# A hybrid decoder step on one core: 320 instead of 344 columns in the RG-LRU, state updates of HGRN2 over 128 stacked rows, and cached keys scored two blocks at a time with a ring of eleven

## The chip, the core and the metric

One core of one Trainium2 chip (trn2) runs the whole program. The metric is the device time of one execution in microseconds.

## What is computed

A four-layer trunk runs over one prompt of 256 tokens and over eight sampled sequences of 8 tokens, 320 columns in all, with the model dimension 1024 and everything in float32. Layers 0 and 3 have an RG-LRU mixer, layer 1 an SSD mixer, layer 2 an HGRN2 mixer; behind each mixer stands a cross attention of 4 heads into 256 memory tokens. For the prompt the memory's keys and values are computed here; for the eight samples they are read from a cache (`cache_mem_k`, `cache_mem_v`). What the change touches, cut from the reference:

```python
# causal_conv: y is the sum of four taps over the columns and the state of 3 columns in front
uu = jnp.concatenate([state, u], axis=1)
y = b + sum(w[k] * uu[:, k:k + L] for k in range(4))
# rglru_mixer, 2048 channels in 8 blocks of 256
r = sigmoid(blocks(u) @ w_a + b_a)
i = sigmoid(blocks(u) @ w_x + b_x)
log_a = -8.0 * r * softplus(-lam)
a = exp(log_a)
b = sqrt(-expm1(2.0 * log_a)) * (i * u)
h = scan(h_t = a_t * h_(t-1) + b_t)         # from h0 for each sequence
y = (h * silu(gate)) @ w_out
# gla_chunked of hgrn2_mixer, 16 heads, key and value dimension 128; for a sample of 8 tokens one chunk
G = cumsum(log_f)
o = causal(q exp(G) (k exp(-G))^T) v + q exp(G) S
S = S * exp(G_last) + (k * exp(G_last - G))^T v
# memory_cross_attn
p = softmax(q mem_k^T / 16)
y = (p mem_v) @ w_o
```

## The kernel before

**Layout.** The columns 0 to 255 (SEQ) are the prompt, 256 to 319 the samples, sequence by sequence; NT is 320. Inside the RG-LRU and the SSD there is a second layout of 347 columns, in which each sample sequence has its 3 columns of convolution state in front of it (SEG = 11 columns a sequence). CV is 344, the width over which the convolution and what follows it run in that layout.

**Weights.** SyncE (SP) brings each weight block (8 x 256 columns for all 128 partitions) into one of 4 slots of `raw`, four DMAs each (`put`), and waits for a slot to come free. ScalarE rounds it to fp32r halves `wh` (line 1613), GpSimd makes the remainder `wl` (line 1593, eight instructions a block). TensorE makes every projection as three fp32r products, high x high (line 751), low x high (line 752) and high x low (line 756), of 320 columns each, 8 chunks deep. Each engine's program is written out by hand, in the order in which the lines stand, and the engines wait for each other by counting semaphores. `did` counts an instruction of VectorE's own, `sync` waits until the counted ones have ended.

**RG-LRU.** A layer has 8 groups of 256 channels. TensorE's loop takes for each group the gate (`take_gate`, which waits for VectorE's line 2300 to have read the gate before), u (`take_u`), and the two fp32 gate products of the convolved u for the group before (`take_ri`, line 842: 8 products of CV columns, 16 records; it waits for the end of the convolution, `rg_conv_done`, and for the packed state output to be read), then `turn_pack`, which transposes the new states. VectorE runs `conv` (line 2284 the first tap, line 2288 the other three, two instructions a tap), `gate` (2300), `update` (2304, 2306), `scan` (2312 to 2320), `product` (2329 for the 256 prompt columns, 2330 for the 64 sample columns, which it gathers from the layout with gaps) and `o_low` (2332 on). ScalarE does the sigmoids (lines 1690 to 1716), Exp, Ln and the rounding of the output. The copy to a transposed output is read at line 2133 (`outs`).

**HGRN2.** A layer has 8 groups, each a pair of heads. TensorE takes g, q, f and v of group i (`take_g`, `take_q`, `take_f`, `take_v`) and between them works on group j = i - 1. `turn_and_score` makes transposes of the keys (bank 5), and the scores (line 1209). `turn_back` (line 1202) transposes on and waits for VectorE's copy of the keys. The state of the eight samples of a head is updated by

```python
def gain(i, h, half):
    if half == 0:
        pe.wait_ge(*past("hg_vm_ready", i * 2 + (h + 1)))
    if i + h + half:
        pe.wait_ge(*past("hg_sn_read", i * 4 + (2 * h + half)))
    v = hg_vm[64:P, 4 * half:4 * half + 4, :]
    pe.matmul(ps[:, 7, :], hg_kt[64:P, 2, :], v, start=True, stop=True).then_inc(S("hg_sn_full"), 1)
```

an fp32 product over the 64 sample rows, of 4 sequences x 128 columns; the trace has two records for one such product. `hg_vm` holds the v of the 64 tokens laid out by sequence with zeros elsewhere (VectorE, lines 2630 to 2635), `hg_kt` the keys turned to rows, copied out of PSUM (line 2604). VectorE adds each gain to the decayed state (`new_state`, 2623 to 2628; `hg_sn_read` counts them). TensorE's order in one iteration is take_g, take_q 0, turn_and_score 0, take_q 1, turn_back 0, gain(j,0,0), take_f 0, outputs and last_state of head 0, take_f 1, turn_and_score 1, gain(j,0,1), take_v 0, turn_back 1, take_v 1, gain(j,1,0), outputs and last_state of head 1, take_v 2, gain(j,1,1), sums. ScalarE (from line 1935) reads the projections: line 1956 for one of q's and k's sources, 1975 and 1976 for v, and the exponentials in between. VectorE then has masks, blocks of v, sums of logs, keys, new states, `finish` (2637) and the gate in that order (loop at 2714 to 2750).

**Attention.** The 16 cached key blocks of a layer (128 tokens x 1024, two for each of 8 samples) and then its 16 value blocks come by one DMA of 512 KB each into a ring of 12 buffers, `at_kb`; load n waits for `at_kb_used` of n - 12. Six of the ring's first seven are loaded early (`EARLY`), the seventh (`kb5`) behind `h_ready`, the other five with the query weights. TensorE turns each key block in 8 transposes (line 1427), ScalarE and VectorE copy four each into one of two buffers `at_kbt`, and the block's 8 score products (32 rows each, 128 columns, line 1437, two records each) stand behind the transposes of the next block:

```python
for n in range(1, 16):
    turn_cache(n)
    cache_scores(n - 1)
    if n in (5, 6, 11, 12):
        prompt_turn(n // 8, (n - 5) % 6)
cache_scores(15)
```

Then the values are multiplied with the probabilities, 4 products a block (line 1505), and SP loads the last four value blocks as the first four are used. SP also stores the prompt's new keys (`store_keys`).

## Time and profile before

| | |
|---|---|
| time, median of 3 runs (range) | 2144.67 us (2142.47 to 2145.44) |
| the profiled execution's own time | 2145.3 us |
| its span in the trace | 2143.4 us |
| mean granted TensorE clock | 0.963 |
| DMA | 324.36 MB, mean 151 GB/s |

The trace shows when each instruction of each engine ran, what it read and wrote by the program's names, and, where its engine stood idle before it, which instruction released it. PE is TensorE, DVE VectorE, ACT ScalarE, POOL GpSimd. A line in the order of time is a run of like instructions: the start of the first, the time from it to the end of the last (instructions of one engine overlap somewhat), the number, and in brackets the idle time before the first and its releaser. PEclk is the granted TensorE clock as a share of the full 2.4 GHz. An fp32 product of TensorE has two records in the trace, an fp32r product one.

### The profile page before, as it was taken

Reading aid. Unit: us, or ns where it says so; the run is one execution under the profiler, and the core shown is the slowest. Engines: PE = TensorE matmul, PEld = TensorE weight load, DVE = VectorE, ACT = ScalarE, POOL = GpSimd, SP = SyncE. Lnnn points to the kernel's source line nnn. Section 1 sums busy time; section 2 is a strip of 40 time slices with the busy share of each in tenths; the row PEclk is TensorE's granted clock in tenths of the full one; section 3 lists DMA queues with packets and bytes.
Section 4 is the critical chain, followed back from the end, with each engine's and each line's share of the span. In section 5 each row is a group of like instructions: output and inputs, shape, how many; then the busy total and the mean of one; then the engine's idle time right before and its main releaser. Section 6 shows DMA issues by size and latency. Waiting matters only on the chain.

```text
span 2143.4 us, 35491 instructions
## 1 busy us (share of the span) xinstructions
PE 2010.6 (94%) x13874; PEld 1788.5 (83%) x13874; DVE 1242.6 (58%) x2220; ACT 905.9 (42%) x1501; POOL 994.8 (46%) x1245
## 2 busy tenths in 40 slices
PE   5898999998999999999999999998999999989987
PEld 4887989698888898897898888887898888879966
DVE  6688442426787777744256566666354147873443
ACT  3476522333544444333353343333242347663332
POOL 4667705036445554150365455555432347665602
PEclk8999999999999999999999999999899999999997
DMA  4443466635434445475452344444386344435850
GB/s 126 132 136 125 133 214 229 213 99 163 117 109 132 134 133 153 161 256 189 131 169 75 112 130 125 135 136 135 103 289 205 135 147 132 142 119 168 280 203 25
DMA packets 331590, 324.36 MB, mean 151 GB/s; under 512 B 21560, under 2 KB 312288, under 8 KB 331424
## 3 DMA queue, kind: packets, MB, share of 16 engines
q1 hardware_dynamic: 330560, 321.75, 47.0%
q8 instruction: 111, 1.82, 0.3%
q10 hardware_dynamic: 864, 0.34, 0.1%
q14 instruction: 55, 0.45, 0.1%
HBM read 292.41 MB, written 29.61 MB: 150 GB/s over the span
## 4 chain that ended last, share of the span: by engine, by line
PE 63%; DVE 25%; ACT 5%; issue 3%; DMA 2%; SPq 1%; POOL 0%; ACTq 0%; DVEq 0%
PE ps L751 9%; PE ps L752 9%; PE ps L756 8%; PE ps L1361 5%; PE ps L1370 4%; DVE work L2288 3%; DVE work L2133 2%; PE ps L741 2%; DVE work L2418 2%; PE ps L1427 2%; PE ps L742 2%; PE ps L743 2%; PE ps L1168 2%; PE ps L1444 1%; PE ps L1474 1%
## 5 line engine op out<-in xcount | busy, mean ns | idle before, releaser
L1593 POOL TENSOR_TENSOR wl<-raw,wh 128x256 fp32r<-128x256 f32 x1216 | 990.3, 848 | 1115.1 <-ACT wh L1613 1114.7
L751 PE MATMUL ps<-Hh,wh 128*128 128x320 f32 x1280 | 400.2, 326 | 25.2 <-DVE Hl L2172 12.2
L1613 ACT ACTIVATE wh<-raw 128x1024 fp32r<-128x1024 f32 x304 | 311.8, 1053 | 193.4 <-PE ps L756 52.9
L752 PE MATMUL ps<-Hl,wh 128*128 128x320 f32 x1280 | 385.2, 314 | 0.0
L751 PEld LDWEIGHTS ps<-Hh,wh 128*128 128x128 f32 x1280 | 246.2, 192 | 48.5 <-issue 24.2
L752 PEld LDWEIGHTS ps<-Hl,wh 128*128 128x128 f32 x1280 | 246.7, 193 | 1.5
L2133 DVE TENSOR_SCALAR work<-ps 128x512 f32<-128x512 f32 (+9 forms) x236 | 108.1, 474 | 208.1 <-DMA out_rgh_s<-work 50.9
L756 PE MATMUL ps<-Hh,wl 128*128 128x320 f32 x1280 | 215.1, 310 | 0.0
L756 PEld LDWEIGHTS ps<-Hh,wl 128*128 128x128 f32 x1280 | 196.1, 189 | 0.0
L751 PE MATMUL ps<-Oh,wh 128*128 128x320 f32 x512 | 156.8, 318 | 3.7 <-DVE Ol L2859 3.7
L752 PE MATMUL ps<-Ol,wh 128*128 128x320 f32 x512 | 155.6, 316 | 0.0
L741 PE MATMUL ps<-Oh,wh 128*128 128x320 f32 x400 | 126.3, 316 | 3.5 <-POOL wl L1593 1.4
L2190 DVE TENSOR_TENSOR work<-work 128x320 f32<-128x320 f32 x80 | 41.1, 514 | 143.4 <-ACT work L2099 112.4
L742 PE MATMUL ps<-Ol,wh 128*128 128x320 f32 x400 | 123.9, 310 | 0.0
L743 PE MATMUL ps<-Oh,wl 128*128 128x320 f32 x400 | 123.8, 309 | 0.0
L1361 PE MATMUL ps<-work,raw 128*128 128x256 f32 x512 | 113.8, 379 | 0.0
L1370 PE MATMUL ps<-raw,work 128*128 128x256 f32 x512 | 113.3, 379 | 0.0
L1370 PEld LDWEIGHTS ps<-raw,work 128*128 128x128 f32 x512 | 96.8, 190 | 13.5
L1361 PEld LDWEIGHTS ps<-work,raw 128*128 128x128 f32 x512 | 96.5, 190 | 13.5
L751 PEld LDWEIGHTS ps<-Oh,wh 128*128 128x128 f32 x512 | 99.7, 195 | 4.9 <-DVE Ol L2859 4.8
L752 PEld LDWEIGHTS ps<-Ol,wh 128*128 128x128 f32 x512 | 99.5, 194 | 0.0
L842 PE MATMUL ps<-work,raw 128*128 128x344 f32 x256 | 81.4, 472 | 15.9 <-DVE work L2133 15.3
(412 smaller groups left out, 3809.4 us busy)
## 6 DMA issues: line engine op xcount, KB each, us to landing
raw<-rg_w_in SPq DMA_DIRECT2D x128, 256.0 KB, 3.6
raw<-hg_w_in SPq DMA_DIRECT2D x128, 256.0 KB, 4.8
raw<-ssd_w_in SPq DMA_DIRECT2D x96, 256.0 KB, 4.0
work<-cache_mem_k SPq DMA_DIRECT2D x40, 512.0 KB, 6.0
raw<-rg_w_out SPq DMA_DIRECT2D x64, 256.0 KB, 3.5
raw<-x_w_k SPq DMA_DIRECT2D x64, 256.0 KB, 3.6
raw<-x_w_v SPq DMA_DIRECT2D x64, 256.0 KB, 3.5
raw<-x_w_q SPq DMA_DIRECT2D x64, 256.0 KB, 5.4
```

The source lines that it names most:

```text
L741: pe.matmul(out, high(*wi), mh, start=start, stop=False)
L742: pe.matmul(out, high(*wi), ml, start=False, stop=False)
L743: return pe.matmul(out, low(*wi), mh, start=False, stop=stop)
L751: pe.matmul(ps[:, bank, 0:n], high(half, k), mh[:, k, 0:n], start=(k == 0), stop=False)
L752: pe.matmul(ps[:, bank, 0:n], high(half, k), ml[:, k, 0:n], start=False, stop=False)
L756: mm = pe.matmul(ps[:, bank, 0:n], low(half, k), mh[:, k, 0:n], start=False, stop=(k == 7))
L842: mm = pe.matmul(ps[:, 4 + 2 * m + j, 0:CV], w, rg_u[i % 2][:, k, 0:CV], start=(k == 0), stop=(k == 1))
L1361: mm = pe.matmul(ps[:, n % 4, 0:NMEM], raw[:, block % SLOTS, k, n % 2 * P:(n % 2 + 1) * P], memh[:, k, :], start=(k == 0), stop=(k == KD - 1))
L1370: mm = pe.matmul(ps[:, bank, 256 * a:256 * a + 256], memh[:, k, a * P:(a + 1) * P], raw[:, block % SLOTS, k, :], start=(k == 0), stop=(k = ...
L1593: ins = pool.tensor_tensor(out, src, wh[:, parted(n) % HALVES, r:r + 2].bitcast(F32), ALU.subtract)
L1613: act.activation(wh[:, nx.n % HALVES], raw[:, slot, :, half * P:(half + 1) * P], ACT.Copy).then_inc(hi_ready, 1)
L2133: return ts(out, src, 1.0, None, MUL)
```

## The change

Three parts, independent of each other.

**RG-LRU.** The first three taps of the convolution still run over 344 columns, into a new buffer `rg_w`. The last tap writes the 320 columns without the gaps, so it is four instructions, for each of two channel blocks one of 256 columns and one of 64. The gate products (line 842), the sigmoids, the exponentials, the update, the scans and the product run over 320 columns; the product is one instruction of 2 x 320 columns instead of two. Helpers for the layout with gaps (`by_seq`, `apart`) go.

**HGRN2.** The gain becomes two fp32r products of 512 columns over 128 rows. Rows 64 to 127 of `hg_v` hold v of the samples as before, rows 0 to 63 hold its low part (v minus v rounded to fp32r), and `hg_vm` is laid out for both halves. The keys are turned twice, so that the 64 rows stand twice, and split in a high part `hg_kp[:, 0]` and a low part `hg_kp[:, 1]` (two VectorE instructions and their syncs, counted by `hg_kp_ready`, for which gain waits). ScalarE copies v into rows 64 to 127, rounds it into `hg_vh`, waits for itself and issues a DMA that copies the rows to 0 to 63; VectorE waits for it (`hg_v_twice`) and subtracts. The last gain of a group, gain(j,1,1), stands in the next group's `take_g` instead of behind `take_v 2`.

**Attention.** Two key blocks of one sample are scored together by 8 products of 256 columns, four of them (the even chunks) behind the transposes of one block and four (the odd chunks) behind the next, one pair late. There are two pairs of buffers, carved from an area that the stored keys use before, so the copies of block 2 wait for the stores. The ring loses `kb5` and has 11 buffers; SP's wait for `h_ready` with its one load goes, and five loads instead of four wait for `at_kb_used`.

```diff
@@ -353,7 +359,9 @@
-hg_v, hg_vm, hg_kt = c(3, 256), c(NB, P), c(3, P)
+hg_v = c(3, 256)
+c(NB + 4, P)
+hg_kt, hg_kx = c(2, P), par[:, 3, :]
@@ -362,14 +370,15 @@
-at_kbt = c(2, KD, P)
+c(2, KD, P)
...
-kb5 = c(D)
+c(D)
...
+at_kbt = [work[:, at:at + 2048].rearrange("p (n c m) -> p n c m", n=2, c=KD) for at in (0, 4096)]
@@ -377,8 +386,8 @@
-at_kb = [c(D), c(D), c(D), work2[:, 3072:4096], work2[:, 4096:5120], gate_area[:, 0:D], kb5]
-EARLY, SQUARES = 6, 7
+at_kb = [c(D), c(D), c(D), work2[:, 3072:4096], work2[:, 4096:5120], gate_area[:, 0:D]]
+EARLY = 6
@@ -661,16 +670,13 @@
-    for n in range(SQUARES, CACHED):
+    for n in range(EARLY, CACHED):
...
-    sp.wait_ge(*past("h_ready", KD * (2 * layer + 2)))
-    for n in range(EARLY, SQUARES):
-        cache(n)
@@ -839,7 +845,7 @@
-                    mm = pe.matmul(ps[:, 4 + 2 * m + j, 0:CV], w, rg_u[i % 2][:, k, 0:CV], start=(k == 0), stop=(k == 1))
+                    mm = pe.matmul(ps[:, 4 + 2 * m + j, 0:NT], w, rg_u[i % 2][:, k, :], start=(k == 0), stop=(k == 1))
@@ -1145,6 +1151,8 @@
+        if i >= 2:
+            gain(i - 2, 1, 1)
@@ -1180,7 +1188,8 @@
-        pe.transpose(ps[:, 5, 256:384], hg_k[:, h, NT - P:NT], ident[:]).then_inc(S("hg_kt_full"), 1)
+        pe.transpose(ps[:, 5, 256:384], hg_k[:, h, NT - P:NT], ident[:])
+        pe.transpose(ps[0:64, 5, 256:384], hg_k[:, h, SEQ:NT], ident[:]).then_inc(S("hg_kt_full"), 1)
@@ -1217,8 +1226,11 @@
-        v = hg_vm[64:P, 4 * half:4 * half + 4, :]
-        pe.matmul(ps[:, 7, :], hg_kt[64:P, 2, :], v, start=True, stop=True).then_inc(S("hg_sn_full"), 1)
+        if half == 0:
+            pe.wait_ge(*past("hg_kp_ready", i * 2 + (h + 1)))
+        v = hg_vm[:, 4 * half:4 * half + 4, :]
+        pe.matmul(ps[:, 7, :], hg_kp[:, 0, :], v, start=True, stop=False)
+        pe.matmul(ps[:, 7, :], hg_kp[:, 1, :], v, start=False, stop=True).then_inc(S("hg_sn_full"), 1)
@@ -1304,10 +1316,10 @@
-        gain(j, 1, 1)
...
+    gain(6, 1, 1)
@@ -1427,16 +1439,18 @@
-    def cache_scores(n):
-        b, a = n // 2, n % 2
-        pe.wait_ge(*past("at_kbt0_ready", seen + n + 1))
-        pe.wait_ge(*past("at_kbt1_ready", seen + n + 1))
-        at = 256 * (b // 4) + P * a
-        for c in (0, 2, 4, 6, 1, 3, 5, 7):
+    def cache_scores(b, odd):
+
+        if odd == 0:
+            pe.wait_ge(*past("at_kbt0_ready", seen + 2 * b + 2))
+            pe.wait_ge(*past("at_kbt1_ready", seen + 2 * b + 2))
+        at = 256 * (b // 4)
+        for c in range(odd, KD, 2):
...
-            mm = pe.matmul(ps[rows, 7, at:at + P], at_qz[:, b, c, :], at_kbt[:, n % 2, c, :],
-                           start=(n == 0 and c % 2 == 0), stop=(n == 15 and c % 2 == 1), skip_group_check=True)
-        mm.then_inc(S("at_cs_full"), 1)
+            mm = pe.matmul(ps[rows, 7, at:at + 256], at_qz[:, b, c, :], at_kbt[b % 2][:, :, c, :],
+                           start=(b == 0 and odd == 0), stop=(b == NB - 1 and odd == 1), skip_group_check=True)
+        if odd:
+            mm.then_inc(S("at_cs_full"), 1)
@@ -1458,13 +1472,15 @@
+    turn_cache(1)
...
-    for n in range(1, 16):
+    for n in range(2, 16):
...
-        cache_scores(n - 1)
+        cache_scores((n - 2) // 2, n % 2)
...
-    cache_scores(15)
+    cache_scores(NB - 1, 0)
+    cache_scores(NB - 1, 1)
@@ -1687,33 +1706,33 @@
-            steps.did(act.activation(rg_r[:, j, 0:CV], ps[:, 4 + j, 0:CV], ACT.Sigmoid, bias=column(1, j)))
+            steps.did(act.activation(rg_r[:, j, 0:NT], ps[:, 4 + j, 0:NT], ACT.Sigmoid, bias=column(1, j)))
...
@@ -1973,7 +1992,11 @@
-        act.activation(hg_v[:, 2, :], ps[:, a + 1, 0:256], ACT.Copy).then_inc(S("hg_v_read"), 1)
+        act.activation(hg_v[64:P, 2, :], ps[64:P, a + 1, 0:256], ACT.Copy).then_inc(S("hg_v_read"), 1)
+        act.wait_ge(*past("hg_v_read", i + 1))
+        steps.did(act.activation(hg_vh[64:P], hg_v[64:P, 2, :], ACT.Copy))
+        steps.sync()
+        act.dma_start(hg_v[0:64, 2, :], hg_v[64:P, 2, :]).then_inc(S("hg_v_twice"), 16)
@@ -2061,9 +2084,12 @@
-        if n >= 2:
-            act.wait_ge(*past("at_cs_full", seen + n - 1))
-        act.activation(at_kbt[:, n % 2, 0:4, :], ps[:, 4, :].rearrange("p (c m) -> p c m", c=4), ACT.Copy).then_inc(S("at_kbt0_ready"), 1)
+        if n == 2:
+            for h in range(2):
+                act.wait_ge(*past(f"at_k_out{h}", (L + 1) * 32))
+        if n >= 4:
+            act.wait_ge(*past("at_cs_full", 8 * L + (n - 4) // 2 + 1))
+        act.activation(at_kbt[n // 2 % 2][:, n % 2, 0:4, :], ps[:, 4, :].rearrange("p (c m) -> p c m", c=4), ACT.Copy).then_inc(S("at_kbt0_ready"), 1)
@@ -2281,15 +2307,19 @@
-            did(ts(u[:, j, 0:CV], own[:, j, 0:CV], tap(0, j), rgc[:, 0, l, 2 * i + j:2 * i + j + 1], MUL, ADD))
-        for k in range(1, 4):
+            did(ts(rg_w[:, j, 0:CV], own[:, j, 0:CV], tap(0, j), rgc[:, 0, l, 2 * i + j:2 * i + j + 1], MUL, ADD))
+        for k in range(1, 3):
...
-                ins = stt(u[:, j, 0:CV], own[:, j, k:k + CV], tap(k, j), u[:, j, 0:CV], MUL, ADD)
-                if k == 3 and j == 1:
-                    ins.then_inc(S("rg_conv_done"), 1)
-                else:
-                    did(ins)
+                did(stt(rg_w[:, j, 0:CV], own[:, j, k:k + CV], tap(k, j), rg_w[:, j, 0:CV], MUL, ADD))
+        sync()
+        for j in range(2):
+            did(stt(u[:, j, 0:SEQ], own[:, j, 3:SC], tap(3, j), rg_w[:, j, 0:SEQ], MUL, ADD))
+            ins = stt(u[:, j, SEQ:NT].rearrange("p (b s) -> p b s", b=NB), samples(own, SC)[:, j, :, 3:SEG], tap(3, j), samples(rg_w, SC)[:, j, :, 0:NL], MUL, ADD)
+            if j:
+                ins.then_inc(S("rg_conv_done"), 1)
+            else:
+                did(ins)
@@ -2301,33 +2331,32 @@
-        did(tt(rg_i[:, :, 0:CV], rg_i[:, :, 0:CV], rg_u[i % 2][:, :, 0:CV], MUL))
+        did(tt(rg_i, rg_i, rg_u[i % 2], MUL))
-            did(dve.tensor_tensor_scan(rg_r[:, j, 0:CV], rg_a[:, j, 0:CV], rg_i[:, j, 0:CV], 0.0, MUL, ADD))
+            did(dve.tensor_tensor_scan(rg_r[:, j, :], rg_a[:, j, :], rg_i[:, j, :], 0.0, MUL, ADD))
-        did(tt(rg_o[:, :, 0:SEQ], rg_r[:, :, 0:SEQ], g[:, :, 0:SEQ], MUL))
-        tt(by_seq(rg_o), apart(rg_r), by_seq(g), MUL).then_inc(S("rg_o_done"), 1)
+        tt(rg_o, rg_r, g, MUL).then_inc(S("rg_o_done"), 1)
@@ -2601,11 +2628,16 @@
-        copy(hg_kt, ps[:, 5, 0:384].rearrange("p (t c) -> p t c", t=3)).then_inc(S("hg_kt_read"), 1)
+        did(copy(hg_kx, ps[:, 5, 256:384]))
+        copy(hg_kt, ps[:, 5, 0:256].rearrange("p (t c) -> p t c", t=2)).then_inc(S("hg_kt_read"), 1)
+        sync()
+        did(copy(hg_kp[:, 0, :], hg_kx))
+        sync()
+        tt(hg_kp[:, 1, :], hg_kx, hg_kp[:, 0, :].bitcast(F32), SUB).then_inc(S("hg_kp_ready"), 1)
...
-        tt(hg_att[h][sm, SEQ:NT], ps[sm, 4, SEQ:NT], s_causal[sm], MUL).then_inc(S("hg_att_ready"), 1)
+        tt(hg_att[h][0:64, SEQ:NT], ps[0:64, 4, SEQ:NT], s_causal[0:64], MUL).then_inc(S("hg_att_ready"), 1)
@@ -2629,10 +2661,12 @@
-            wait("hg_v_read", i + 1)
+            wait("hg_v_twice", 16 * (i + 1))
+            did(tt(hg_v[sm, 2, :], hg_v[sm, 2, :], hg_vh[sm].bitcast(F32), SUB))
+            sync()
...
-        tt(hg_vm[sm], hg_v[sm, 2, h * P:(h + 1) * P].unsqueeze(1).broadcast_to([64, NB, P]), wide(s_block[sm, :], P), MUL).then_inc(S("hg_vm_ready"), 1)
+        tt(hg_vm[:], hg_v[:, 2, h * P:(h + 1) * P].unsqueeze(1).broadcast_to([P, NB, P]), wide(s_block[:], P), MUL).then_inc(S("hg_vm_ready"), 1)
@@ -2817,9 +2851,12 @@
-        if n >= 2:
-            wait("at_cs_full", 16 * L + n - 1)
-        copy(at_kbt[:, n % 2, 4:8, :], ps[:, 5, :].rearrange("p (c m) -> p c m", c=4)).then_inc(S("at_kbt1_ready"), 1)
+        if n == 2:
+            for h in range(2):
+                wait(f"at_k_out{h}", (L + 1) * 32)
+        if n >= 4:
+            wait("at_cs_full", 8 * L + (n - 4) // 2 + 1)
+        copy(at_kbt[n // 2 % 2][:, n % 2, 4:8, :], ps[:, 5, :].rearrange("p (c m) -> p c m", c=4)).then_inc(S("at_kbt1_ready"), 1)
```

## Rows read from the trace of the kernel before

**Rows 1.** The page's busy time of each engine over the span.
```profile
PE 2010.6 (94%) x13874; PEld 1788.5 (83%) x13874; DVE 1242.6 (58%) x2220; ACT 905.9 (42%) x1501; POOL 994.8 (46%) x1245
```
**Rows 2.** Order of time, TensorE, first RG-LRU: start us, us, what [idle before].
```profile
92.04 4.89 PE L842 MATMUL ps<-work,raw 128*128 128x344 f32 x16
...
96.51 0.57 PE L751 MATMUL ps<-Hh,wh 128*128 128x320 f32 x1
...
99.11 1.33 PE L756 MATMUL ps<-Hh,wl 128*128 128x320 f32 x8
...
137.01 0.41 PE L751 MATMUL ps<-Hh,wh 128*128 128x320 f32 x1 [0.83 <-DVE work L2300]
...
157.62 0.42 PE L751 MATMUL ps<-Hh,wh 128*128 128x320 f32 x1 [0.84 <-DVE work L2300]
...
213.81 6.27 PE L842 MATMUL ps<-work,raw 128*128 128x344 f32 x16 [7.45 <-DVE work L2133]
```
**Rows 3.** The same view, VectorE, one group of the first RG-LRU.
```profile
136.89 1.25 DVE L2329 TENSOR_TENSOR work<-work 128x512 f32<-128x512 f32 x1
138.06 0.83 DVE L2330 TENSOR_TENSOR work<-work 128x128 f32<-128x128 f32 x1
...
142.49 5.45 DVE L2288 SCALAR_TENSOR_TENSOR work<-work,par 128x344 f32<-128x344 f32 x6
...
153.08 0.88 DVE L2312 TENSOR_TENSOR work<-work 128x688 f32<-128x688 f32 x1 [1.42 <-ACT work L1716]
153.87 0.17 DVE L2314 TENSOR_TENSOR work<-work 128x16 f32<-128x16 f32 x1
```
**Rows 4.** The same view: line 2314 in an earlier group, and GpSimd.
```profile
90.40 0.71 DVE L2314 TENSOR_TENSOR work<-work 128x16 f32<-128x16 f32 x1
...
146.56 4.04 POOL L1593 TENSOR_TENSOR wl<-raw,wh 128x256 fp32r<-128x256 f32 x4 [0.58 <-ACT wh L1613]
```
**Rows 5.** Order of time, TensorE, one group of HGRN2.
```profile
1287.51 0.38 PE L1202 MATMUL ps<-work 128*128 128x128 f32 x2
1288.92 1.12 PE L1221 MATMUL ps<-work 64*128 64x512 f32 x2
1289.97 0.42 PE L751 MATMUL ps<-Hh,wh 128*128 128x320 f32 x1
...
1302.84 0.39 PE L1168 MATMUL ps<-wh,Hh 128*128 128x256 f32 x1 [0.15 <-ACT work L1956]
...
1306.96 0.33 PE L1209 MATMUL ps<-work,later 128*64 128x64 f32 x2
...
1311.65 1.12 PE L1221 MATMUL ps<-work 64*128 64x512 f32 x2 [1.30 <-DVE work L2635]
...
1321.18 1.12 PE L1221 MATMUL ps<-work 64*128 64x512 f32 x2 [0.59 <-DVE work L2628]
...
1338.81 0.38 PE L1202 MATMUL ps<-work 128*128 128x128 f32 x2
```
**Rows 6.** The same view, VectorE: the copy of the turned keys.
```profile
1337.90 0.55 DVE L2133 TENSOR_SCALAR work<-ps 128x384 f32<-128x384 f32 x1
```
**Rows 7.** Order of time, TensorE: scores of cached keys; SSD's 256-column products.
```profile
399.15 0.65 PE L1437 MATMUL ps<-work 128*32 128x128 f32 x16
399.72 1.09 PE L1427 MATMUL ps<-ident,work 128*128 128x128 f32 x8
...
867.43 1.07 PE L1025 MATMUL ps<-work 128*32 128x256 f32 x16 [1.55 <-ACT work L1827]
868.43 0.70 PE L1006 MATMUL ps<-work 128*128 128x256 f32 x2
```
**Rows 8.** Order of time, TensorE: two of the last value blocks.
```profile
423.69 0.64 PE L1505 MATMUL ps<-work 128*32 128x256 f32 x8 [0.22 <-DMA work<-cache_mem_v]
...
425.00 0.64 PE L1505 MATMUL ps<-cache_area,work 128*32 128x256 f32 x8 [0.67 <-DMA cache_area<-cache_mem_v]
```
**Rows 9.** Busy time by stretch: stretch, us, engines, PEclk, DMA share, GB/s.
```profile
1300.00:1320.00 20.00, 18.55 (x150) 16.17 (x149) 11.32 (x23) 8.22 (x15) 9.55 (x11) 0.91 0.35 106
```

59 lines of the change are left out of this document (32 added, 27 removed).

## The prediction

> **What bounds the kernel now.** I read the page first, then TensorE's waits, then the order of time in one group of each mixer and in one scoring stage. TensorE is busy for 94% of the span [rows 1], so a microsecond taken from its work is worth a microsecond wherever nobody else sets the pace. The question is where that holds: in both recurrent mixers TensorE waits for VectorE in every group [rows 2, 5].
>
> In the RG-LRU, TensorE stands still before 137.01 and 157.62, 0.83 and 0.84 us each, because `take_gate` waits for line 2300, and for 7.45 us in front of the last gate product [rows 2]. The two waits are one group apart, 20.6 us, and VectorE is full for all of it but two short waits for ScalarE, the second of them 1.42 us [rows 3]. So the period is VectorE's chain: gate, product, low part, convolution, update, scan, gate.
>
> In HGRN2, follow TensorE from the last score product (line 1209, starting at 1306.96) to `turn_back` of the next pair of heads (line 1202, 1338.81) [rows 5]: 31.5 us from the end of the one to the start of the other. In the same stretch VectorE goes through the masks, the blocks of v, the sums of logs, the keys, the new state, `finish` and the gate, and ends the copy that `turn_back` waits for at 1337.90 + 0.55 = 1338.45 [rows 6]. From 1307.3 that is 31.1 us: TensorE's path and VectorE's path are level to 0.4 us. I call this stretch A, the rest of the group (1287.51 to 1307.3, 19.8 us) stretch B; together 51.3 us.
>
> **RG-LRU, 320 columns.** TensorE: the 16 records of one block's gate products take 96.51 - 92.04 = 4.47 us at 344 columns [rows 2]; 320 make it 4.16, 0.31 less, 5.0 us over 16 groups. Nearly all of it only lengthens the waits of 0.84 us, so it is costed at nothing while VectorE sets the period. The last block of each mixer comes behind a 7.45 us wait and runs at half clock (213.81, its 16 records last 5.8 us): there 0.4 us are real, 0.8 together.
>
> VectorE, per group. (a) The gated product was two instructions, 1.25 and 0.83, together 2.0 us with their overlap [rows 3]; one of 640 columns should take 1.4 (the 1.25 of 512 columns and 128 more at 1 ns: 688 columns take 0.88 and 16 take 0.17): -0.6. (b) The last tap was a third of 5.45, 1.82 us for two instructions. It becomes four, two of 256 and two of 64 columns. What a short one costs depends on GpSimd: a 16-column product takes 0.17 us at 153.87 and 0.71 at 90.40, and GpSimd is at work from 146.56 to 150.60, which is where the last tap runs [rows 3, 4]. Bounds for the four: 2 x 0.40 + 2 x 0.17 = 1.15 (nobody in the way) and 2 x 0.82 + 2 x 0.71 = 3.05 (each one delayed). I take 2.4, +0.6, nearer to the upper end, since the neighbouring taps show the delayed length (0.91 each); some of the delay is given back, because GpSimd's four instructions are over sooner and the update behind them then runs free. (c) 24 or 48 columns fewer in the update, the first product of the scan, the scans and ScalarE's Ln and Exp: about 1 ns a column, -0.35. Sum -0.35 us a group (bounds -1.6 and +0.3). Some six groups in each of the two RG-LRU layers run at VectorE's pace: -4.2. RG-LRU in all: -5.0 (bounds -20, where TensorE's own path would stop it near -13, and +3).
>
> The Trainium skill has a rule that speaks against this part (SBUF — State Buffer, Who interferes with whom): a VectorE instruction with two SBUF inputs and a reading GpSimd instruction exclude each other for the whole instruction. By it every extra short instruction can wait once more, and the last tap costs its upper end, 3.05 us. The trace agrees as far as rows 4 go.
>
> **HGRN2, stacked gains.** The gain was one fp32 product of 512 columns over 64 rows, two records; from its start to the next product 1289.97 - 1288.92 = 1.05 us [rows 5]. Now there are two fp32r products of 512 columns. Eight fp32r products of 320 columns take 1.33 us, the last of them lasting 0.31 [rows 2], so they follow each other at 0.146 us and 512 columns cost about 0.23, two of them 0.45: -0.6 per gain, 32 gains, 19 us on paper. Moving gain(j,1,1) into the next `take_g` also takes its wait of 0.59 [rows 5] off TensorE. Per group:
>
> Stretch B holds gain(j,0,0), in the open: -0.6. It needs `hg_kp_ready`, two more VectorE instructions and two syncs behind `hg_kt_read`, about 0.8 us (bounds 0.6 and 1.4), and is covered by `turn_back` itself, 1288.92 - 1287.51 = 1.4 us. It also holds gain(j,0,1), but that one is hidden now: `take_v` behind it already waits 0.15 us for ScalarE's line 1956 [rows 5], which depends on the scores in front of the gain. Shortening it only makes that wait 0.7. The added transpose stands in front of the scores: +0.1. B: -0.5.
>
> Stretch A holds the other two gains and the moved wait: TensorE's path falls by 0.6 + 0.6 + 0.59 = 1.8. But VectorE's path grows: the low part of v (64 rows x 256) with its sync, 0.42 by the column price above and 0.54 more where GpSimd delays it (the 0.71 against the 0.17), I take 0.45 since GpSimd rests there; the extra copy `hg_kx` in front of `hg_kt_read`, 0.1. So A becomes 31.1 + 0.55 + 0.1 (the semaphore) = 31.75 against 31.5 now: +0.2. The wait of 1.30 us before gain(j,1,0) [rows 5] stays, because it ends with the blocks of v and these follow line 1209. ScalarE's copy to `hg_vh`, its sync and the DMA cost it about 0.7 us behind the v copies; the halves it splits next are needed 7 us later, and the DMA (a few us) has 12 us before VectorE asks for it. Both are costed at nothing; uncovered they would add to A. Six groups: 6 x (-0.5 + 0.2) = -1.8.
>
> The first group (slow clock, TensorE late there) and the last heads among the output products are TensorE's: some seven gains at 0.6, two of them at half clock at 1.1, less 0.5 for the longer VectorE path: -4.3. What replaces the wait: TensorE will stand about 1.9 us in front of turn_back of the first head (its path is 1.8 shorter, VectorE's 0.2 longer). After a wait of 1.30 and the small output products behind it, the granted clock is 0.91 over 1300 to 1320 [rows 9], 3.6 us at half level (1.2 GHz), and so once in each of six groups. A new wait of 1.9 with small products behind it can bring such a stretch into B, where it costs half of its length, 1.7 us. I count two of six: +3.4. HGRN2: -2.7 (bounds -22 and +8).
>
> **Attention, pairs of key blocks, four layers.** The columns streamed are the same: 16 records of 128 before, 8 of 256 now, per key block. 16 records of 128 take 399.72 - 399.15 = 0.57 us, 16 of 256 take 868.43 - 867.43 = 1.00 [rows 7]: 27 and 53 ns a record and 0.15 around them, so 8 of 256 again take 0.58. In the middle nothing changes, and the second pair of buffers takes away no wait that the trace has. The end gets longer: the last two half-calls follow each other, 1.00 instead of 0.57: +0.43. At the start the missing call was hidden behind VectorE's copy. The wait for stored keys at n = 2 is costed at nothing, since the stores go out long before.
>
> The ring goes from twelve to eleven. The loads of the last values wait for the first value block; there were four of them, now five, back to back. The third and the fourth let TensorE start at 423.69 and 425.00 [rows 8]: one more costs 1.3 us, all of it in TensorE's way, as the last block is waited for in every layer. Below it could cost 0 if the block's transfer found a faster path, above 1.5. 4 x (0.43 + 1.3) = 6.9. The longer idle end can stretch one of the four slow clock stretches that follow it: +1.7. Attention: +8.6 (bounds +2 and +14).
>
> **Sum.** -5.0 - 2.7 + 8.6 = +0.9 on the profiled execution's 2145.3 us, which stands 0.6 above the median. That gives 2146 us. A measurement of this kernel can tell about 0.2%, 4.3 us, from no change; so this is no change.
>
> **Rivals.** (1) TensorE's count stands: it is the bound everywhere, and VectorE's chains give way. 5.0 in the RG-LRU, 19.2 and 3.5 in HGRN2, against 6.9: -21, 2124 us. For it speaks the 94%; against it the waits named above. 0.10. (2) The RG-LRU's VectorE chain shortens fully: GpSimd stays out of the last tap's way, -1.0 a group. 12 groups: -12 instead of -4.2, 2138 us. 0.20. (3) The last tap pays for every short instruction, +0.3 a group at the upper end (3.05 us): +3.6 instead of -4.2, 2154 us. It decides from a tap of about 2.9 us on. The page's lock rule is this case. 0.16. (4) The new wait before turn_back brings half clock into every group: six times 1.7 and not two, +6.8, 2153 us, slower; it decides from four groups of six. For it speaks that 1.30 is already enough in stretch A; against it that dense products, not small ones, stand in front of the new wait. 0.16. My forecast keeps 0.38.
>
> The range reaches over (2), (3) and (4) and the bounds of the ring's cost: 2132 to 2159; it leaves out (1) and a combination of (3) and (4). Faster (1, 2) 0.30, no change 0.38, slower (3, 4) 0.32.
>
> **What would show it.** Right: RG-LRU groups still 20 us or more apart with a wait at line 2300; the product at 1.4; HGRN2 groups at 51 us, `turn_back` waiting near 2 us for VectorE's copy and the wait for line 2628 gone; the value products waiting 1.3 us longer per layer. Wrong: HGRN2 groups below 50 us (stretch A isn't VectorE's), RG-LRU groups at 19.3 (the tap is cheap), or a last value block that doesn't wait longer.

## The result and the profile after

The changed kernel takes 2164.32 us (median of 4 runs, 2161.92 to 2169.96); the kernel before took 2143.57 beside it. The ratio is 1.0108, 95% interval 1.0076 to 1.0140: slower by 1.1%, outside the range given. The spans of the two profiled executions differ by 20.8 us (2164.2 and 2143.4), and that is the difference which the traces have to account for. The ratios go by fast executions alone; of e5's twelve below, one took 5998.93 us and is left out.

First, the engines' busy times over the span after, against [rows 1]:

```profile
PE 2001.2 (92%) x13378; PEld 1788.1 (83%) x13378; DVE 1256.9 (58%) x2286; ACT 907.2 (42%) x1509; POOL 1001.4 (46%) x1249
```

TensorE is busy for 9.4 us less, in a span that is 20.8 longer. So the change did take work from TensorE, and TensorE is idle for 30 us more. The projections are the same 6912 products in both kernels and in the same order, so the starts of a few of them cut both spans into the same stretches (each difference is worked out from two starts):

| stretch | before | after | difference | forecast |
|---|---|---|---|---|
| RG-LRU, layer 0 and layer 3, to the attention's first query product | 301.7 + 256.7 | 299.4 + 252.7 | -6.3 | -5.0 |
| attention from there, four layers | 586.6 | 595.9 | +9.3 | +8.6 |
| HGRN2, from the first `turn_back` of head 0 to the eighth | 364.1 | 386.8 | +22.7 | +1.6 |
| HGRN2's last heads and output products | 105.0 | 99.7 | -5.3 | -4.3 |
| all else | 529.2 | 529.6 | +0.4 | 0 |

Two cautions on reading it. The forecast's -4.3 was for the first group and the last heads together, so a part of it belongs to the third line. And one profiled execution differs from the next where nothing was changed: e3 below leaves HGRN2 as it was, and the layer is 4.3 us shorter in it (514.0 for 518.3, from its first product to the attention's). A few microseconds in one line say little, so four of five lines stand near enough to where the forecast put them, and the miss is in the third. The same two executions over those seven groups, in the table by stretch (stretch, us, busy times of PE, PEld, DVE, ACT and POOL, granted clock, DMA share, GB/s), first before:

```profile
1129.54:1493.62 364.08, 346.16 (x2595) 310.81 (x2595) 232.08 (x377) 139.45 (x222) 192.92 (x228) 0.95 0.38 118
```

and after:

```profile
1131.67:1518.51 386.84, 344.49 (x2610) 322.84 (x2609) 252.34 (x427) 145.13 (x229) 208.45 (x230) 0.92 0.37 113
```

The granted clock is lower, 0.92 for 0.95. What TensorE waits for in them (line, releaser, us in total, times, longest), before:

```profile
PE ps L1221 <- DVE work L2635: 9.1, 7, 1.3
PE ps L1202 <- DVE work L2133: 4.3, 1, 4.3
PE ps L1221 <- DVE work L2628: 3.5, 6, 0.6
PE ps L1168 <- ACT work L1956: 1.1, 7, 0.2
```

and after, where line 1211 is `turn_back` and 1232 the stacked gain:

```profile
PE ps L1211 <- DVE work L2159: 30.9, 7, 5.1
PE ps L1232 <- DVE hg_vm L2669: 4.2, 7, 0.6
PE ps L1176 <- ACT work L1975: 3.8, 7, 0.5
```

`turn_back` waited once, in the last group; now it waits 4.0 to 5.1 us at the end of each of the seven. This is the wait that was forecast with 1.9. One group after in order of time, TensorE (start, us, what, idle before):

```profile
1294.87 0.80 PE L1211 MATMUL ps<-work 128*128 128x128 f32 x2 [4.04 <-DVE work L2159]
1295.46 1.81 PE L1217 MATMUL ps<-ident,sq_area 128*128 128x64 f32 x8
...
1321.84 0.50 PE L1232 MATMUL ps<-hg_vm,hg_kp 128*128 128x512 f32 x1 [0.60 <-DVE hg_vm L2669]
...
1333.90 0.39 PE L1232 MATMUL ps<-hg_vm,hg_kp 128*128 128x512 f32 x1
1334.14 0.39 PE L1233 MATMUL ps<-hg_vm,hg_kp 128*128 128x512 f32 x1
1334.37 0.31 PE L757 MATMUL ps<-Hh,wh 128*128 128x320 f32 x1
...
1351.63 0.80 PE L1211 MATMUL ps<-work 128*128 128x128 f32 x2 [5.12 <-DVE work L2159]
```

The eight transposes behind the wait last 1.81 us; where the clock is full (1316.92 in this trace, 1306.03 in the one before) they last 1.00. The two stretches of the forecast, B (from `turn_back` to the last score product of head 1) and A (from there to the next `turn_back`), in this group:

```profile
1294.87:1318.19 23.32, 22.78 (x163) 21.30 (x163) 5.84 (x15) 8.59 (x12) 8.39 (x13) 0.81 0.43 136
1318.19:1351.63 33.44, 27.22 (x215) 25.42 (x215) 30.49 (x47) 12.39 (x21) 21.71 (x22) 1.00 0.35 105
```

and in the group of [rows 5]:

```profile
1287.51:1307.29 19.78, 19.63 (x164) 17.32 (x162) 5.02 (x10) 9.07 (x13) 11.32 (x17) 1.00 0.59 186
1307.29:1338.81 31.52, 29.63 (x213) 26.94 (x214) 28.09 (x44) 11.06 (x19) 15.61 (x17) 0.95 0.30 89
```

Both are longer. B has its 23.32 us at a granted clock of 0.81. What it takes at full clock shows in the first of the seven groups, which has no wait in front of it:

```profile
1131.67:1151.07 19.40, 18.86 (x164) 17.58 (x163) 5.84 (x15) 9.06 (x13) 11.12 (x17) 1.00 0.18 56
```

So 3.9 us of the 23.32 are the slow clock's. Before, B had the full clock in this group; the slow stretch lay in A, which VectorE's path of 31.1 us held at 31.5 all the same.

The same two stretches added up over the seven groups (the cuts are those of the group shown, the length at half clock is worked out from the granted clock of each stretch):

| seven groups, us | B | of it at half clock | A | of it at half clock |
|---|---|---|---|---|
| before | 140.1 | 3.4 | 224.0 | 31.1 |
| after | 154.6 | 41.9 | 232.2 | 23.0 |
| e7: HGRN2's part, gain(j,1,1) at its old place | 137.1 | 3.4 | 228.0 | 29.0 |
| e2: HGRN2's part as it is | 156.0 | 45.0 | 233.5 | 24.8 |
| e13: e2 with ScalarE's split later | 149.5 | 30.6 | 221.7 | 15.5 |
| e14: e2 with TensorE kept at work | 143.6 | 17.1 | 234.1 | 11.7 |
| e15: both | 138.7 | 6.8 | 221.4 | 13.8 |

(e2 to e15 follow below.) Of the 22.7 us, 14.5 lie in B, and these are the slow clock's: at 19.40 us each, seven of them would take 135.8. The other 8.2 lie in A.

In the group shown, A is 1.9 us longer at full clock, and there VectorE ends last. VectorE at the end of A, first before:

```profile
1333.60 1.22 DVE L2635 TENSOR_TENSOR work<-work,s_block 64x1024 f32<-64x1024 f32 x1
1334.85 1.01 DVE L2641 SCALAR_TENSOR_TENSOR work<-work,par,hg_rs 128x320 f32<-128x320 f32 x2
1335.90 0.49 DVE L2133 TENSOR_SCALAR Oh<-work 128x640 fp32r<-128x640 f32 x1
1336.43 0.82 DVE L2647 TENSOR_TENSOR Ol<-work,Oh 128x640 fp32r<-128x640 f32 x1
```

then after:

```profile
1344.15 0.42 DVE L2665 TENSOR_TENSOR work<-work,hg_vh 64x256 f32<-64x256 f32 x1
1344.61 1.65 DVE L2669 TENSOR_TENSOR hg_vm<-work,s_block 128x1024 fp32r<-128x1024 f32 x1
1346.17 1.94 DVE L2675 SCALAR_TENSOR_TENSOR work<-work,par,hg_rs 128x320 f32<-128x320 f32 x2
1348.15 0.90 DVE L2159 TENSOR_SCALAR Oh<-work 128x640 fp32r<-128x640 f32 x1
1349.09 1.23 DVE L2681 TENSOR_TENSOR Ol<-work,Oh 128x640 fp32r<-128x640 f32 x1
```

The low part of v (0.42) is as forecast. But everything behind it is 0.41 to 0.47 us an instruction longer, though `finish`, the last four instructions, is no part of the change: 4.1 us for 2.3, the lengths added up. GpSimd in the same stretch, before and after:

```profile
1336.85 5.84 POOL L1593 TENSOR_TENSOR wl<-raw,wh 128x256 fp32r<-128x256 f32 x8 [6.76 <-ACT wh L1613]
```

```profile
1344.38 7.90 POOL L1612 TENSOR_TENSOR wl<-raw,wh 128x256 fp32r<-128x256 f32 x8 [3.75 <-ACT wh L1632]
```

Before, GpSimd's eight instructions begin when `finish` is nearly over. After, they begin with VectorE's blocks of v and cover all of `finish`, and they are longer themselves, 7.90 for 5.84. They follow ScalarE's split of the weights, before and after:

```profile
1335.72 2.00 ACT L1613 ACTIVATE wh<-raw 128x1024 fp32r<-128x1024 f32 x2
```

```profile
1343.26 2.00 ACT L1632 ACTIVATE wh<-raw 128x1024 fp32r<-128x1024 f32 x2
```

The split stands behind the scores of the next head: TensorE, freed of its wait, has these ready sooner, and the split starts 25.1 us after A begins and no longer 28.4. VectorE does not wait for the product that was moved: its addition of that gain starts at 1343.43, 9 us behind the product, right after the instruction before it.

The parts that came out as forecast, shortly. RG-LRU, VectorE after, against [rows 3]:

```profile
135.44 1.39 DVE L2359 TENSOR_TENSOR work<-work 128x640 f32<-128x640 f32 x1
...
144.33 0.85 DVE L2317 SCALAR_TENSOR_TENSOR work<-work,par 128x256 f32<-128x256 f32 x1
145.10 0.76 DVE L2318 SCALAR_TENSOR_TENSOR work<-work,par 128x64 f32<-128x64 f32 x1
145.79 0.98 DVE L2317 SCALAR_TENSOR_TENSOR work<-work,par 128x256 f32<-128x256 f32 x1
146.69 0.77 DVE L2318 SCALAR_TENSOR_TENSOR work<-work,par 128x64 f32<-128x64 f32 x1
```

The product is at 1.4, and the last tap takes its upper bound, 3.1 us (144.33 to 147.4), with all four instructions delayed. The next gate begins 20.14 us after the one before (20.6 in [rows 2]), still behind a wait for VectorE's gate. The update behind the taps gave a part back: its second instruction is at 0.81 (149.39) where it took 1.41 on average before.

### The profile page after: what moved, and what is told of

The parts are those of the page before. It is cut to its first block, busy times and chain, and to the rows that moved or that the text cites. A ratio compares the mean times of both kernels' runs of the same rounds, so it can differ in the third digit from the quotient of the medians.

```text
span 2164.2 us, 34546 instructions
## 1 busy us (share of the span) xinstructions
PE 2001.2 (92%) x13378; PEld 1788.1 (83%) x13378; DVE 1256.9 (58%) x2286; ACT 907.2 (42%) x1509; POOL 1001.4 (46%) x1249
## 4 chain that ended last, share of the span: by engine, by line
PE 59%; DVE 26%; ACT 6%; issue 5%; DMA 3%; SPq 1%; ACTq 0%; DVEq 0%
PE ps L757 8%; PE ps L758 7%; PE ps L762 7%; PE ps L1373 5%; PE ps L1382 4%; PE ps L747 3%; PE ps L748 3%; PE ps L749 3%; DVE work L2159 2%; DVE work L2445 2%; DVE work L2314 2%; PE ps L1439 2%; PE ps L1176 1%; ACT wh L1632 1%; PE ps L848 1%
## 5 line engine op out<-in xcount | busy, mean ns | idle before, releaser
L757 PE MATMUL ps<-Hh,wh 128*128 128x320 f32 x1280 | 403.5, 328 | 23.4 <-DVE Hl L2198 13.8
L2159 DVE TENSOR_SCALAR work<-ps 128x512 f32<-128x512 f32 (+8 forms) x236 | 106.2, 467 | 205.4 <-DMA out_rgh_s<-work 52.9
L848 PE MATMUL ps<-work,raw 128*128 128x320 f32 x256 | 77.7, 458 | 19.1 <-DVE work L2159 19.1
```

The costliest lines, as they stand in the source:

```text
L757: pe.matmul(ps[:, bank, 0:n], high(half, k), mh[:, k, 0:n], start=(k == 0), stop=False)
L848: mm = pe.matmul(ps[:, 4 + 2 * m + j, 0:NT], w, rg_u[i % 2][:, k, :], start=(k == 0), stop=(k == 1))
L2159: return ts(out, src, 1.0, None, MUL)
```

## The experiments

All ratios are to the kernel before, run beside on the same chip; its median was 2140.62, 2143.81, 2141.75 and 2141.7 us in the four sets. Runs of different sets are compared by their ratios, times 2142 us. Spans and groups are those of one profiled execution each.

**e1, e2, e3: each part alone.**

> The kernel before with the RG-LRU part of the change alone. The whole change's trace gains 2.3 us over layer 0's RG-LRU and 4.0 over layer 3's. If the parts are independent, this kernel is 6.3 us faster than before (0.997). Rival: the gain belongs to the new memory layout or to a shift of time from the other parts; then it is within 2 us of before.

> The kernel before with the HGRN2 part alone. Theory: all of the loss that was not forecast is here, 17.4 us between the start and the end of layer 2's mixer, so this kernel is 17 us slower than before (1.008), with 4 to 5 us of waiting before each first turn_back of a group and groups 55 us apart. Rival: part of the loss comes from the other parts (a shift of the DMA or of the clock); then it is at most 10 us slower.

> The kernel before with the attention part alone. Theory: 2 to 3 us a layer, 9.3 in all as in the trace of the whole change (1.0043). Rival: the one more value block in the ring is all, 1.3 a layer, 5 in all.

| | median us | ratio (95%) | us against before |
|---|---|---|---|
| RG-LRU | 2137.96 | 0.9979 (0.9964 to 0.9994) | -4.5 |
| HGRN2 | 2155.82 | 1.0070 (1.0051 to 1.0089) | +15 |
| attention | 2152.23 | 1.0052 (1.0033 to 1.0071) | +11 |

The last column is the ratio's distance from 1 times 2141. The three ratios make 1.0101 together, the whole change 1.0108: that is what independent parts would give. The rivals of e2 and e3 lie outside the intervals; e1's (within 2 us of before) just touches its own, 1.3 to 7.7 us faster. HGRN2's part alone has the waits of 4.0 to 5.1 us, 7.0 in the last group, and groups of 55.6 us on average.

**e4 and e5: `finish` out of VectorE's chain**, in the HGRN2 part and in the kernel before.

```diff
                         tt(hg_q[i % 2], hg_q[i % 2], ps[:, 2 - a:4 - a, 0:NT], MUL).then_inc(S("hg_q_read"), 1)
+                    if i >= 2:
+                        finish(i - 2)
                     if i:
                         last_state(i - 1, 0)
...
-                    if i:
-                        finish(i - 1)
+                finish(GROUPS - 1)
```

`gated` of head 0 also waits for `hg_o_ready`, since it writes what `finish` reads.

> The HGRN2 part alone, with VectorE's finish of the pair of heads before taken from in front of turn_back's copy and put behind the product of q, where VectorE stands idle for over 7 us. Theory: VectorE's chain of 33.4 us sets stretch A, 4.1 of it are finish; without it A falls to TensorE's own 29.5 us, the wait of 4 to 5 us and the half clock behind it go, the group takes 49 us instead of 55, and the kernel is 40 us faster than the HGRN2 part alone and 15 to 25 faster than before. Rival 1: TensorE's work itself grew (the stacked products and the extra transpose), then the wait goes elsewhere and the time stays within 5 us of the HGRN2 part alone. Rival 2: the half clock comes from the wait of 0.6 before the stacked gain as well and stays, then 20 to 25 us faster than the HGRN2 part.

> The kernel before with finish moved as in the HGRN2 experiment, no stacked gains. It tells how much of that gain was open before. Theory: TensorE's and VectorE's paths through stretch A are level to 0.4 us in the kernel before, so taking 2.3 us (finish's three lengths there) off VectorE gives 0.4 a group, and the one wait of 4.3 us of the last group with the half clock behind it: 3 to 8 us faster than before. Rival: VectorE alone sets stretch A, 2.3 us in seven groups, 16 us and more. If the first holds, the stacked gains are worth the rest, 18 to 23 us, once VectorE is out of the way.

e4: 2114.31 us, ratio 0.9875 (0.9853 to 0.9897), 26 us faster than before and 41 than e2. e5: 2137.94, ratio 0.9977 (0.9958 to 0.9997), 5 us. The main theory of e4 holds. That of e5 holds in its number, and its last group has lost the wait of 4.3 us, but its seven groups together are no shorter than before (364.5 us for 364.1, at a granted clock of 0.93 for 0.95), so the 5 us do not show where the theory had them. TensorE's waits for VectorE's copy in the seven groups, e2 and then e4:

```profile
PE ps L1213 <- DVE work L2154: 34.8, 7, 7.0
```

```profile
PE ps L1213 <- DVE work L2154: 3.0, 1, 3.0
```

The groups take 346.5 us where e2's take 389.5. So the stacked gains, with their move, are worth some 22 us in the end (e4 against e5), but only when VectorE's chain lets them.

**e6, e7, e9: the move of gain(j,1,1)**, alone on the kernel before, taken back in the HGRN2 part, and taken back in the whole change. e7 and e9 have this diff, e6 its reverse:

```diff
                     project(gfv(i), 0)
-                    if i >= 2:
-                        gain(i - 2, 1, 1)
                     project(gfv(i) + 1, 1)
...
                     take_v(i, 2)
+                    gain(j, 1, 1)
                     sums(j)
...
                 take_out()
-                gain(6, 1, 1)
                 take_out()
```

> The kernel before with gain(j,1,1) alone moved behind the next group's first projection. TensorE's path through A loses its wait of 0.59 us, VectorE's work stays. Theory: 0.4 us a group at most, 0 to 4 us faster than before, and a new wait of 0.2 us in front of turn_back. Rival: a small shift of ScalarE's and GpSimd's work against VectorE's end of the chain already brings the collision (finish at 4.1 instead of 2.3 us) and with it waits of 2 us; then 5 to 15 us slower.

> The HGRN2 part with gain(j,1,1) left where it was before. Theory: VectorE's chain sets stretch A, so TensorE's wait before turn_back gets 0.6 us shorter, one of 0.6 comes back in front of the gain, and the time is that of the HGRN2 part alone within 3 us. Rival: the move is what let ScalarE and GpSimd run ahead into VectorE's end of the chain; then at least 6 us faster than the HGRN2 part alone.

> The whole change with one thing undone: gain(j,1,1) stands behind the third product of v again. Theory from the HGRN2 part with and without the move: the seven groups lose 24 us by the move alone, so this kernel is 20 to 26 us faster than the whole change, within 6 us of before (the RG-LRU 6 and the last heads of HGRN2 6 faster, the attention 9 slower). Rival: the parts together shift the work so that the collision stays; then at least 10 us slower than before.

e6: 2144.54 us, ratio 1.0009 (0.9992 to 1.0025): nothing to be told from no change. It brings a wait of 0.6 us in front of `turn_back` in three groups, and `finish` stays at 2.4 to 2.8 us from its first start to its last end in all but the last group, as before: without the stacked gains the move brings no collision. e7: 2130.82, ratio 0.9945 (0.9928 to 0.9963), 27 us faster than the same part with the move; my theory said within 3 us, and it fell. e9: 2136.27, ratio 0.9978 (0.9960 to 0.9995): the whole change without the move is 5 us faster than before and 28 faster than with it. TensorE's waits in e7's seven groups (line 1232 is the gain, 2652 the state that it waits for, 1211 `turn_back`):

```profile
PE ps L1232 <- DVE work L2652: 17.2, 7, 3.1
PE ps L1211 <- DVE work L2152: 8.5, 4, 5.9
```

TensorE waits for VectorE here too, but 1.5 to 3.1 us of it at the gain, 18 us ahead of `turn_back` (1316.08 and 1334.23), and in front of `turn_back` only 0.8 to 0.9 us in three groups and 5.9 in the last. The groups take 365.1 us at a granted clock of 0.96, and in this group A lasts 31.7 us (1302.52 to 1334.23) with the instructions of e2 on VectorE. What differs is when the slow clock comes and when GpSimd does: `finish` takes 2.4 to 2.8 us from its first start to its last end in six groups, 4.1 in e2's. By the table above, 18.9 of the 24 us between e2's and e7's groups lie in B and 5.5 in A. The next four take the two causes apart.

**e8 and e14: TensorE kept at work in the wait**, e8 in all seven groups (12 without the condition), e14, whose diff this is, in the six that wait. The output does not depend on these products.

```diff
                     take_q(i, 1)
+                    for _ in range(12 if i >= 2 else 0):
+                        pe.matmul(ps[:, 6, 320:512], ident[:], restart[:, 0:192], start=True, stop=True)
                     turn_back(j, 0)
```

**e13: ScalarE's split behind `finish`**, and e15 with both (8 products).

```diff
                         scores_by_query(i - 1, 0)
+                    if i >= 2:
+                        act.wait_ge(*past("hg_o_ready", i - 1))
                     ahead(b + 2)
```

> The HGRN2 part with 12 fp32 products of 192 columns that nobody reads in front of each first turn_back, about 4 us of work in the wait of 4 to 5 us. VectorE's chain is untouched. Theory: 6.8 us at half clock follow each of these waits and cost half their length in stretch B; with TensorE kept at work they go, about 3 us a group, 15 to 20 us faster than the HGRN2 part alone, near the time of before. Rival: the clock is without weight since VectorE sets the pace in B too, or the half clock comes all the same: within 4 us of the HGRN2 part alone.

> The HGRN2 part with the move kept. ScalarE waits for the end of finish before it splits the next weight block, so GpSimd's eight instructions cannot lie beside finish. Theory: finish takes 2.3 us again instead of 4.1, VectorE's chain through A falls from 33.4 to 31.6 us, the wait before turn_back from 4 to 5 down to 2.5 to 3.5; 1.8 us in six groups, 11 us faster than the HGRN2 part alone, more if the half clock shrinks. Rival: finish's length has another cause than GpSimd; then within 3 us of the HGRN2 part alone. A loss would say that the halves come late for take_f.

> As the earlier run with 12 products that nobody reads in front of turn_back, but only in the six groups that have the wait of 4 to 5 us. VectorE's chain stays at 33 us. Theory: the half clock in stretch B goes, the seven groups take 373 us instead of 389 and the kernel is 10 to 15 us faster than the HGRN2 part alone. Rival: what the clock gives back there it takes elsewhere (the earlier run's median did not move), then within 4 us.

> Both: ScalarE's split behind finish, and 8 products that nobody reads in front of turn_back. If the two causes are all there is, the groups come to about 361 to 365 us, as without the move, 22 to 28 us faster than the HGRN2 part alone. If they are one and the same, it is no better than the better of the two.

| HGRN2 part with the move | median us | ratio (95%) | seven groups, us |
|---|---|---|---|
| e2, as it is | 2155.82 | 1.0070 (1.0051 to 1.0089) | 389.5 |
| e8, 12 products in seven groups | 2156.26 | 1.0063 (1.0043 to 1.0084) | 376.4 |
| e14, 12 products in six | 2146.15 | 1.0018 (1.0002 to 1.0034) | 377.7 |
| e13, split late | 2141.40 | 0.9995 (0.9977 to 1.0013) | 371.2 |
| e15, both | 2134.98 | 0.9960 (0.9941 to 0.9979) | 360.2 |
| e7, without the move | 2130.82 | 0.9945 (0.9928 to 0.9963) | 365.1 |

The granted clock over the seven groups, e2 and then e14:

```profile
1125.78:1515.30 389.52, 344.33 (x2610) 322.78 (x2609) 253.38 (x427) 145.19 (x229) 209.02 (x230) 0.91 0.37 112
```

```profile
1128.20:1505.92 377.72, 352.85 (x2753) 331.60 (x2752) 256.01 (x427) 144.97 (x229) 210.58 (x230) 0.96 0.38 116
```

and VectorE at the end of A in e13:

```profile
1334.29 1.22 DVE L2665 TENSOR_TENSOR hg_vm<-work,s_block 128x1024 fp32r<-128x1024 f32 x1
1335.43 1.01 DVE L2671 SCALAR_TENSOR_TENSOR work<-work,par,hg_rs 128x320 f32<-128x320 f32 x2
1336.47 0.49 DVE L2156 TENSOR_SCALAR Oh<-work 128x640 fp32r<-128x640 f32 x1
1337.00 0.83 DVE L2677 TENSOR_TENSOR Ol<-work,Oh 128x640 fp32r<-128x640 f32 x1
```

GpSimd's next eight instructions start behind all of it, at 1339.00. `finish` is back at 2.3 us and the blocks of v at 1.22, so their length had been GpSimd's doing. Keeping the clock up gives 11 us, taking the collision away 16, both 24, nearly the 27 of undoing the move. The two are not quite separate: of the 18.3 us that e13's groups are shorter, 11.8 lie in A and 6.5 in B, since a shorter wait (2.3 to 3.0 us for 4.0 to 5.1) also leaves less of the half clock. e14's gain lies all in B (12.4 us; A is 0.6 longer). e8 missed its forecast in the median though not in the trace: its groups are 13 us shorter, but the products in the first group, which has no wait, are in the way there (53.1 us before the first `turn_back` for 49.3), and the rest of its profiled execution was 7 us longer than e2's at other places. I can't say why beyond the granted clock, which falls at other moments in each execution.

**e12: the ring alone.** The kernel before without `kb5` and with the loads as in the change; keys are scored one block at a time.

```diff
-        at_kb = [c(D), c(D), c(D), work2[:, 3072:4096], work2[:, 4096:5120], gate_area[:, 0:D], kb5]
-        EARLY, SQUARES = 6, 7
+        at_kb = [c(D), c(D), c(D), work2[:, 3072:4096], work2[:, 4096:5120], gate_area[:, 0:D]]
+        EARLY = 6
```

> The kernel before with a ring of eleven buffers (kb5 left out), key blocks scored one by one as before. It splits the attention's 9 us. Theory: the fifth late value block costs 1.0 to 1.3 us a layer, 4 to 5 us slower than before; the pairs are the other 0.5 a layer at the last scores and the slow clock behind. Rival: the seventh early key block was needed (SP's wait for used buffers comes earlier), then 6 us and more.

2152.33 us, ratio 1.0059 (1.0037 to 1.0080): 13 us slower, as much as the whole attention part. The rival's size, not its reason: the waits for the last value blocks over the whole span are, before,

```profile
PE ps L1505 <- DMA cache_area<-cache_mem_v: 4.1, 4, 2.0
PE ps L1505 <- DMA gate_area<-cache_mem_v: 1.5, 1, 1.5
PE ps L1505 <- DMA work<-cache_mem_v: 1.2, 4, 0.6
```

and with eleven buffers

```profile
PE ps L1502 <- DMA cache_area<-cache_mem_v: 10.6, 13, 2.0
```

3.8 us more, about 1 a layer; no key block is waited for in either, so the rival's reason is not there. The two profiled executions differ by only 6.1 us, 5.9 of them in the four attention stretches, at a granted clock of 0.960 for 0.963. The rest of the difference between the medians (8 to 17 us by the interval) isn't in these two traces, and whether it belongs to the ring isn't settled. That the pairs save anything shows nowhere: with them the part costs the same, and TensorE waits 3.1 us more for the copies of turned keys (8.6 us in e3, 5.5 in e12). Pairs with a ring of twelve were not tried, since the second pair of buffers lies where `kb5` was.

**e10 and e11: the parts that help, together.** Both have the RG-LRU and the HGRN2 part with `finish` late and the attention of before; e11 has gain(j,1,1) at its old place.

> RG-LRU part and HGRN2 part with the move and with finish behind the product of q; attention as before. The two gains measured alone add up: 4 to 6 and 26 us, so 30 to 33 us faster than before (0.985). Rival: they share a part (the clock, layer 3's start), then 24 to 28.

> As the run before, but gain(j,1,1) at its old place. Theory: once finish is out of VectorE's chain, TensorE sets the pace, and the old place only adds the wait for line 2628's successor to TensorE's path: 0 to 5 us slower than with the move. Rival: the move is bad in itself (its 24 us come from the place in take_g, not from VectorE's chain), then it is 15 to 25 us faster than with the move.

e10: 2112.12 us, ratio 0.9867 (0.9843 to 0.9890), the fastest of all, 28 us faster than before and some 50 than the change; the forecast of 30 to 33 lies within its interval. e11: 2118.08, ratio 0.9886 (0.9862 to 0.9909). With `finish` out of the chain the move is no harm any more, as the theory had it: e11 is 4 us slower by the ratios, with overlapping intervals, and its groups take 360.4 us where e10's take 347.2 (the whole spans differ by 2.6 us only). The RG-LRU's gain can't be seen in e10 beside e4; their intervals are wider than it.

## Why the prediction was wrong

**RG-LRU: right.** -5.0 forecast, -6.3 in the traces, -4.5 alone. The number was right in part by luck. The last tap went to its upper bound, 3.1 where 2.4 was taken, and rival (3) would have had the part lose by it. What is left of the 0.47 us that the group gained (20.61 to 20.14) came to -1.2 where (c) had -0.35, half of it the update's second instruction, which ran free of GpSimd. The forecast named this give-back but had it too small, and the two misses cancel. The rule that the prediction cites from the Trainium skill (SBUF — State Buffer, Who interferes with whom), that such instructions of VectorE and GpSimd exclude each other, would have the last tap cost its upper end. The trace agrees: 3.1 us for 3.05.

**Attention: right in the trace** (+9.3 for +8.6), though not term by term: the waits for the last blocks grew by 3.1 us in all (9.9 for 6.8), 0.8 a layer where 1.3 was taken; the scores at the end take 1.00 us (401.78 to 402.78 in e3) for 0.57, as forecast; and 4.5 us are left where 1.7 was put down for the slow clock. "In the middle nothing changes" was wrong: before the transposes of cached keys TensorE waits 3.1 us more, first before and then after,

```profile
PE ps L1427 <- ACT work L2066: 3.3, 8, 0.5
PE ps L1427 <- DVE work L2133: 2.2, 4, 0.6
```

```profile
PE ps L1439 <- ACT work L2092: 4.5, 12, 0.5
PE ps L1439 <- DVE work L2159: 4.1, 11, 0.6
```

and only with the pairs: e3 has the same 8.6 us, e12 the 5.5 of before. So too short a term for the middle and too long a one for the ring nearly cancel. The ring, run alone, costs more in its median than these traces show (e12).

**HGRN2's gains and last heads: right.** The two products and the step to the next take 0.47 us (1333.90 to 1334.37) for the 0.45 forecast, and the last heads gain 5.3 us. The -4.3 was itself added up wrongly: five gains at 0.6 and two at 1.1, less 0.5, are 4.7.

**HGRN2, stretch A: the step that failed first.** "TensorE's path falls by 0.6 + 0.6 + 0.59 = 1.8 ... VectorE's path grows ... A becomes 31.75." A took 33.0 to 33.5 us in all seven groups. The wait at `turn_back` was foreseen, and VectorE's new instructions were costed well (0.42 for 0.45). What was missed is that a shorter path of TensorE moves ScalarE and GpSimd too, because the split of the next weights stands behind the scores. "0.45 since GpSimd rests there" was read off the trace of before, where GpSimd rests until `finish` is nearly over; what the other case costs stood in [rows 4]. It was taken as a property of the place and was one of the time. e13 shows it: the same order with GpSimd held back has A at 31.3 to 31.4 us in five of its seven groups, some 2 us less than e2's 33.1 to 33.5. A smaller miss goes the same way: the wait in front of gain(j,1,0), which "stays" at 1.30, fell to 0.60, so TensorE reached `turn_back` 0.7 us sooner than forecast.

**HGRN2, stretch B: rival (4), and more than it.** This is the larger part of the miss in microseconds: +14.5 where the forecast had +0.4 (six times -0.5, and 3.4). I counted half clock in two of six groups at 1.7 us. It came in all six, at 2.6 to 3.9 us (B of 22.0 to 23.3 us against 19.40 at full clock), behind a wait of 4 to 5 us and not of 1.9. So the two misses feed each other: the collision makes the wait longer. Rival (4) had the mechanism, at half the price. e14 shows the clock's share: 12.4 us come back in B.

**The move.** It was entered as a gain of 0.59 a group. With the stacked gains TensorE has to wait for VectorE in each group, wherever the order puts it (25.7 us over e7's seven groups, 34.8 over e2's). At its old place the gain takes most of this wait early, ahead of the projections, where it holds ScalarE and GpSimd back as well. Moving the gain moved the whole wait in front of `turn_back`, where the half clock behind it falls into B, and let GpSimd into VectorE's end. This one step costs 28 us in the whole change (e9), more than the 21 us that the change loses in all, and nothing without the stacked gains (e6): it is the two together that cost. Without the move the kernel takes 2136 us, inside the range; but the forecast was for the kernel with it.

## What to carry to other kernels

When two engines are level over a stretch, a microsecond taken from the one only moves its wait: ask where the wait lands, what stands behind it, and which engines its old place held back. Cost a VectorE instruction by where GpSimd will be after the change and not where it was, and see whether work that nobody waits for soon can leave the chain first; here that alone turned the stacked gains from 15 us lost into 26 gained, some 5 of which the old gains had with it too (e5).

## What the runs showed of the hardware

At the end of stretch A, GpSimd's instructions with two inputs from SBUF added about the same time to each VectorE instruction beside them, whatever its length: 1.22 to 1.65 us for 1024 columns, 0.82 to 1.23 for 640, and 0.49 to 0.90 for a plain copy of 640 columns, which has one input only. That copies can be delayed so, too, the Trainium skill says (SBUF — State Buffer, Who interferes with whom), for copies in a mode that uses both ports. Whether this copy runs in such a mode no view shows; the trace agrees by 0.41 us. And 12 products that nobody reads, put in the waits of 4 to 5 us, kept the granted clock of seven groups at 0.96 where it was 0.91, and made the program 11 us faster (e14). With 12 more in a group that had no wait, nothing was left of it in the median (e8).
